# First two tiles of five stages multiplied before the input is normalised

## The reference

```python
def rms_norm(x, g, eps=NORM_EPS):
    xf = x.astype(jnp.float32)
    y = xf * lax.rsqrt(jnp.mean(xf * xf, axis=-1, keepdims=True) + eps)
    return (y * g.astype(jnp.float32)).astype(x.dtype)

for l in range(DEPTH):
    x = x + 0.5 * swiglu(rms_norm(x, ffn_norm[l, 0]), ...)      # ffn0, ffn2
    p = rms_norm(x, mix_norm[l]) @ w_in[l]                      # att_in, rec_in
    ...
    x = x + jnp.concatenate([ya, yb, yc], axis=-1) @ w_out[l]   # mix_out
    x = x + 0.5 * swiglu(rms_norm(x, ffn_norm[l, 1]), ...)      # ffn1, ffn3
```

## Time and profile before

| what | value |
| --- | --- |
| median of 3 runs | 3910.22 us (3909.51 to 3916.24) |
| profiled execution | 3910.8 us, its span 3909.0 us |
| mean granted TensorE clock | 0.946 |
| PE busy | 3678.5 us (94%) |
| DVE, ACT, POOL busy | 1465.1, 1211.4, 1237.4 us (37%, 31%, 32%) |
| matmuls of L1642 to L1644 on h, 2736 each | 1079.5, 1067.0, 1067.2 us busy |

### The profile page before, as it was taken

The page is one execution under the profiler, slowest core; times in us unless marked ns, Lnnn a source line. Parts: engine busy times, 40 slices in busy tenths (PEclk is TensorE's granted clock), DMA queues, the critical chain, the costliest instruction groups (busy, mean ns, idle before and its releaser), DMA issues.

```text
span 3909.0 us, 47618 instructions
## 1 busy us (share of the span) xinstructions
PE 3678.5 (94%) x17904; PEld 3033.3 (78%) x17904; DVE 1465.1 (37%) x2601; ACT 1211.4 (31%) x1800; POOL 1237.4 (32%) x516
## 2 busy tenths in 40 slices
PE   8999997689999999999768999989899999989999
PEld 7888775578888888877558888877677888778887
DVE  4430496753330333039565333122454221222110
ACT  3222335223222322233533322222323332323331
POOL 3444330003444344433000244423101444323443
PEclk9999997799999999999768999989999999999999
DMA  4442220003442344222000244322101222212222
GB/s 171 145 145 91 71 81 6 1 1 117 143 145 101 124 145 145 92 71 81 11 1 1 94 144 145 108 76 74 39 6 44 92 97 97 70 54 86 97 97 92
DMA packets 93534, 332.09 MB, mean 85 GB/s; under 512 B 10432, under 2 KB 12128, under 8 KB 93280
## 3 DMA queue, kind: packets, MB, share of 16 engines
q1 hardware_dynamic: 77136, 274.65, 20.3%
q10 hardware_dynamic: 16272, 55.65, 4.2%
HBM read 327.64 MB, written 2.62 MB: 84 GB/s over the span
## 4 chain that ended last, share of the span: by engine, by line
PE 89%; DVE 6%; ACT 2%; issue 1%; DMA 1%; SPq 0%; DVEq 0%; ACTq 0%
PE ps L1642 23%; PE ps L1644 22%; PE ps L1643 22%; PE ps L1676 2%; PE ps L1661 1%; PE ps L1662 1%; PE ps L1666 1%; PE ps L2347 1%; PE ps L1749 1%; DMA w_raw<-in_tiles 1%; PE ps L1901 1%; PE ps L2332 1%; PE ps L1742 1%; PE ps L2080 1%; PE ps L2062 1%
## 5 line engine op out<-in xcount | busy, mean ns | idle before, releaser
L418 POOL TENSOR_TENSOR w_lo<-w_raw,w_hi 128x1024 fp32r<-128x1024 f32 x512 | 1237.2, 2418 | 2648.3 <-ACT w_hi L440 2647.9
L1642 PE MATMUL ps<-h_hi,w_hi 128*128 128x512 f32 x2736 | 1079.5, 395 | 9.0 <-DVE mem L1529 7.0
L1644 PE MATMUL ps<-h_hi,w_lo 128*128 128x512 f32 x2736 | 1067.2, 390 | 0.0
L1643 PE MATMUL ps<-h_lo,w_hi 128*128 128x512 f32 x2736 | 1067.0, 390 | 0.0
L440 ACT ACTIVATE w_hi<-w_raw 128x1024 fp32r<-128x1024 f32 x512 | 541.7, 1058 | 1121.1 <-DMA w_raw<-in_tiles 1121.0
L1642 PEld LDWEIGHTS ps<-h_hi,w_hi 128*128 128x128 f32 x2736 | 514.8, 188 | 130.8 <-issue 14.7
L1643 PEld LDWEIGHTS ps<-h_lo,w_hi 128*128 128x128 f32 x2736 | 514.8, 188 | 108.4 <-issue 3.8
L1644 PEld LDWEIGHTS ps<-h_hi,w_lo 128*128 128x128 f32 x2736 | 514.6, 188 | 108.5
L1009 DVE TENSOR_TENSOR a_lo<-sil,a_hi 128x512 f32 x132 | 275.6, 2088 | 468.4 <-ACT a_hi L516 468.4
L1642 PE MATMUL ps<-a_hi,w_hi 128*128 (+1 forms) x1056 | 415.0, 393 | 0.0
L1643 PE MATMUL ps<-a_lo,w_hi 128*128 (+1 forms) x1056 | 414.3, 392 | 0.0
(11 more groups left out here) (418 smaller groups left out, 3756.5 us busy)
## 6 DMA issues: line engine op xcount, KB each, us to landing
w_raw<-in_tiles SPq DMA_DIRECT2D x512, 512.0 KB, 3.2
ada_raw<-in_ada_tiles ACTq DMA_DIRECT2D x96, 512.0 KB, 3.3
x<-in_x_t SPq DMA_DIRECT2D x2, 1024.0 KB, 6.4
sq<-in_cond ACTq DMA_DIRECT2D x4, 512.0 KB, 4.2
out_t<-x SPq DMA_DIRECT2D x1, 2048.0 KB, 7.1
consts<-in_consts SPq DMA_DIRECT2D x1, 1280.0 KB, 12.6
mem<-in_ctx_t ACTq DMA_DIRECT2D x1, 1024.0 KB, 5.8
core_mem<-in_consts ACTq DMA_DIRECT2D x1, 576.0 KB, 3.7
```

The source lines that it names most:

```text
L418: nc.gpsimd.tensor_tensor(w_lo[:, s, :], w_raw[:, s, :], w_hi[:, s, :].bitcast(F32), ALU.subtract).then_inc(S["w_lo_ready"], 1)
L1642: nc.tensor.matmul(bank, wh, hi, start=first, stop=False, skip_group_check=True)
L1643: nc.tensor.matmul(bank, wh, lo, start=False, stop=False, skip_group_check=True)
L1644: return nc.tensor.matmul(bank, wl, hi, start=False, stop=last, skip_group_check=True)
```

## The change

In att_in0, ffn1, ffn2, att_in1 and ffn3, tiles 1 and 2 are multiplied with x times gain, split in hi and lo but without the norm's factor (`raw_tiles`). ACT makes the hi part (`raise_raw`), DVE the lo part (`lower_raw`), for the first chunks early: four in the middle of the down half of the stage before, or six among the tiles of mix_out. After a feed-forward stage they lie in h_hi and h_lo, after mix_out in a part of a_lo. The sum of the last chunk comes after the first raw chunk, the spreading of the factor after the third. The factor is copied to SBUF, and the normalised h is made beside the raw products, for tiles 3 and 4, which now run side by side. The raw results are scaled afterwards: in a feed-forward stage by two products of DVE around the silu, in attention by one product for each tile. In ACT's loop over h_hi, tile 5 is rounded after the fifth chunk and tile 6 after the seventh. Not shown below: the new semaphores, and the slot of `sil`, which goes by the position of a chunk and no longer by its number.

```diff
@@ -294,6 +294,33 @@
+RAW_NEXT = {"ffn0": "att_in0", "mix_out0": "ffn1", "ffn1": "ffn2", "ffn2": "att_in1", "mix_out1": "ffn3"}
+RAW = {after: name for name, after in RAW_NEXT.items()}
+def raw_parts(name):
+    if RAW[name].startswith("ffn"):
+        return h_hi, h_lo
+    return a_lo[:, 6:6 + KD, :], a_lo[:, 6 + KD:6 + 2 * KD, :]
+def raw_order(name):
+    return FFN_ORDER if RAW[name].startswith("ffn") else tuple(range(KD))
+def raw_gain(name, k):
+    n = int(name[-1])
+    return param("ffn_g" if name.startswith("ffn") else "mix_g", KD * n + k)
+def raw_rstd(name):
+    return mem[:, 27 if name.startswith("ffn") else 47, :]
@@ -450,6 +478,34 @@
+    def raise_raw(name, k):
+        nc.scalar.activation(raw_parts(name)[0][:, k, :], x[:, k, :], ACT.Copy, scale=raw_gain(name, k)).then_inc(S["raw_hi"], 1)
+    def norm_raw(name, updates):
+        order, base = raw_order(name), BASE[name]
+        for n in range(seen.pop("early"), KD):
+            square_x(n, order[n], updates)
+        todo = order[seen.pop("raw_early"):]
+        for k in todo[:len(todo) // 2]:
+            raise_raw(name, k)
+        act.wait_ge(S["ss_ready"], seen["sq_slot"])
+        nc.scalar.activation(rtok[:, :], ps[:, 7, 0:TB], ACT.Sqrt, scale=1.0 / D, bias=eps(EPS_NORM)).then_inc(S["std_ready"], 1)
+        for k in todo[len(todo) // 2:]:
+            raise_raw(name, k)
+        for t in seen.pop("late_tiles"):
+            round_tile(t)
+        for n, k in enumerate(order):
+            act.wait_ge(S["hf_ready"], due("hf_ready"))
+            if n < KD - 1:
+                act.wait_ge(S["raw_used"], due("raw_used"))
+            else:
+                act.wait_ge(S["w_used"], base + 2)
+            nc.scalar.activation(h_hi[:, k, :], sil[:, n % 2, :], ACT.Copy).then_inc(S["h_hi_ready"], 1)
+            if n in (4, 6):
+                round_tile(base + 4 + (n - 4) // 2)
@@ -466,31 +522,38 @@
-    def round_out(base, updates):
+    def round_out(base, updates, after=None):
...
                 square_x(k - 1, k - 1, updates + 1)
+                if after:
+                    raise_raw(after, k - 1)
+        seen["raw_early"] = KD - 2
...
     def ffn(n, order, updates, shift=None):
-        base = BASE[f"ffn{n}"]
-        norm_x(order, updates, shift=shift)
+        name = f"ffn{n}"
+        base, raw, after = BASE[name], name in RAW, RAW_NEXT.get(name)
+        if raw:
+            norm_raw(name, updates)
+        else:
+            norm_x(order, updates, shift=shift)
@@ -500,20 +563,31 @@
                 nc.scalar.activation(row, row, ACT.Silu).then_inc(S["cond_ready"], 1)
-        with act.Fori(0, NF // 2) as i:
+        def pairs(i):
...
-                act.wait_ge(S["w_used"], base + 4 * i + (2 * j + 2))
+                from_raw = raw and isinstance(i, int) and j == 0
                 act.wait_ge(S["a_ready"], NF * n + 2 * i + (j + 1))
-                nc.scalar.activation(sil[:, j, :], ps[:, 2 * j, :], ACT.Silu).then_inc(S["silu_ready"], 1)
-                round_tile(base + 4 + 2 * j, i)
-                round_tile(base + 5 + 2 * j, i)
+                if from_raw:
+                    act.wait_ge(S["raw_scaled"], due("raw_scaled"))
+                    nc.scalar.activation(sil[:, 0, :], sil[:, 0, :], ACT.Silu).then_inc(S["silu_ready"], 1)
+                else:
+                    act.wait_ge(S["w_used"], base + 4 * i + (2 * j + 2))
+                    nc.scalar.activation(sil[:, j, :], ps[:, 2 * j, :], ACT.Silu).then_inc(S["silu_ready"], 1)
+                    round_tile(base + 4 + 2 * j, i)
+                    round_tile(base + 5 + 2 * j, i)
...
+        if raw:
+            pairs(0)
+        with act.Fori(int(raw), NF // 2) as i:
+            pairs(i)
@@ -533,7 +607,10 @@
                 square_x(c, FFN_ORDER[c], updates + 1)
-            seen["early"] = KD // 2
+            if after:
+                for c in range(KD // 2):
+                    raise_raw(after, FFN_ORDER[c])
+            seen["early"] = seen["raw_early"] = KD // 2
@@ -564,8 +641,9 @@
             act.wait_ge(S["w_used"], base + m + 1)
-            nc.scalar.activation(mem[:, att_unit(m), :], ps[:, m % 2, :], ACT.Copy).then_inc(S["proj_out"], 1)
-            round_tile(base + m + 4)
+            nc.scalar.activation(mem[:, att_unit(m), :], ps[:, 4 + m if m < 2 else m % 2, :], ACT.Copy).then_inc(S["proj_out"], 1)
+            if m >= 2:
+                round_tile(base + m + 4)
@@ -775,7 +853,7 @@
         round_h(range(4, KD))
-        round_out(BASE[f"mix_out{l}"], updates)
+        round_out(BASE[f"mix_out{l}"], updates, RAW_NEXT[f"mix_out{l}"])
@@ -969,17 +1047,32 @@
-    def norm_x(gain, shift=None):
+    def lower_raw(name, k):
+        hi, lo = raw_parts(name)
+        dve.wait_ge(S["raw_hi"], due("raw_hi"))
+        nc.vector.scalar_tensor_tensor(lo[:, k, :], x[:, k, :], raw_gain(name, k), hi[:, k, :].bitcast(F32), ALU.mult, ALU.subtract).then_inc(S["raw_lo"], 1)
+    def norm_x(gain, shift=None, raw=None):
+        todo = raw_order(raw)[seen.pop("raw_early"):] if raw else ()
+        for k in todo[:len(todo) // 2]:
+            lower_raw(raw, k)
...
         nc.vector.reciprocal(rtok[:, :], rtok[:, :]).then_inc(S["rtok_ready"], 1)
+        for k in todo[len(todo) // 2:]:
+            lower_raw(raw, k)
...
+        rstd = raw_rstd(raw) if raw else ps[:, 7, :]
+        if raw:
+            link(nc.vector.tensor_copy(rstd, ps[:, 7, :]))
         def make(k, slot):
-            return nc.vector.scalar_tensor_tensor(slot, x[:, k, :], gain(k), ps[:, 7, :], ALU.mult, ALU.mult)
-        split_h(range(KD), make, shift)
+            return nc.vector.scalar_tensor_tensor(slot, x[:, k, :], gain(k), rstd, ALU.mult, ALU.mult)
+        split_h(raw_order(raw) if raw else range(KD), make, shift)
@@ -995,16 +1088,25 @@
     def ffn(n, gain, shift, gate):
-        base = BASE[f"ffn{n}"]
-        norm_x(gain, shift)
+        name = f"ffn{n}"
+        base, raw, after = BASE[name], name in RAW, RAW_NEXT.get(name)
+        norm_x(gain, shift, name if raw else None)
...
             for j in range(2):
-                dve.wait_ge(S["silu_ready"], NF * n + 2 * i + (j + 1))
-                nc.vector.tensor_tensor(sil[:, j, :], sil[:, j, :], ps[:, 2 * j + 1, :], ALU.mult).then_inc(S["af_ready"], 1)
+                if raw and isinstance(i, int) and j == 0:
+                    dve.wait_ge(S["h_ready"], seen["h_hi_ready"])
+                    dve.wait_ge(S["w_used"], base + 2)
+                    nc.vector.tensor_tensor(sil[:, 0, :], ps[:, 0, :], raw_rstd(name), ALU.mult).then_inc(S["raw_scaled"], 1)
+                    dve.wait_ge(S["silu_ready"], NF * n + 1)
+                    link(nc.vector.tensor_tensor(sil[:, 0, :], sil[:, 0, :], ps[:, 1, :], ALU.mult))
+                    nc.vector.tensor_tensor(sil[:, 0, :], sil[:, 0, :], raw_rstd(name), ALU.mult).then_inc(S["af_ready"], 1)
+                else:
+                    dve.wait_ge(S["silu_ready"], NF * n + 2 * i + (j + 1))
+                    nc.vector.tensor_tensor(sil[:, j, :], sil[:, j, :], ps[:, 2 * j + 1, :], ALU.mult).then_inc(S["af_ready"], 1)
@@ -1014,7 +1116,9 @@
                 activations(i, 2)
-        with dve.Fori(both, NF // 2) as i:
+        if raw:
+            activations(0, 1)
+        with dve.Fori(max(both, int(raw)), NF // 2) as i:
@@ -1034,7 +1138,10 @@
+            if half and after:
+                for k in FFN_ORDER[0:KD // 2]:
+                    lower_raw(after, k)
+        seen["raw_early"] = KD // 2
@@ -1063,13 +1170,18 @@
-        norm_x(lambda k: param("mix_g", KD * l + k))
+        norm_x(lambda k: param("mix_g", KD * l + k), raw=f"att_in{l}")
...
         first = seen.get("proj_out", 0)
-        dve.wait_ge(S["proj_out"], first + 1)
+        dve.wait_ge(S["proj_out"], first + 2)
+        rstd = raw_rstd(f"att_in{l}")
+        for unit in (U_KI, U_MISC):
+            ins = nc.vector.tensor_tensor(mem[:, unit, :], mem[:, unit, :], rstd, ALU.mult)
+        ins.then_inc(S["raw_evened"], 1)
+        dve.wait_ge(S["raw_evened"], l + 1)
@@ -1473,6 +1585,9 @@
             V.tensor_tensor(x[:, k, :], x[:, k, :], ps[:, (k - 1) % KD, :], ALU.add).then_inc(S["x_ready"], 1)
+            if 0 < k < KD - 1:
+                lower_raw(RAW_NEXT[f"mix_out{l}"], k - 1)
+        seen["raw_early"] = KD - 2
@@ -1683,14 +1798,46 @@
         seen["early"] = 0
+        spread_rstd()
+    def spread_rstd():
...
+    def raw_tiles(name, banks):
+        (hi, lo), t = raw_parts(name), BASE[name]
+        for n in range(seen.get("early", 0), KD - 1):
+            sum_chunk(n)
+        pe.wait_ge(S["w_lo_ready"], t + 2)
+        for n, k in enumerate(raw_order(name)):
+            block = slice(k * P, (k + 1) * P)
+            pe.wait_ge(S["raw_hi"], due("raw_chunk"))
+            for r in range(2):
+                nc.tensor.matmul(ps[:, banks[r], :], w_hi[:, (t + r) % RING, block], hi[:, k, :], start=(n == 0), stop=False, skip_group_check=True)
```

(37 more changed lines are left out.)

13 lines of the change are left out of this document (7 added, 6 removed).

## The result

| what | before | changed |
| --- | --- | --- |
| median | 3911.52 us (3909.51 to 3917.66, 7 runs) | 3929.29 us (3923.93 to 3944.55, 7 runs) |
| ratio | | 1.0049, 95% interval 1.0033 to 1.0065 |
| profiled execution, its span | 3910.8, 3909.0 us | 3944.55, 3942.8 us |
| mean granted TensorE clock | 0.946 | 0.940 |
| PE busy | 3678.5 us | 3700.4 us |

The change made the kernel 0.5% slower. The forecast of 3917.6 us had the sign and the place; its size was off by 11.7 us, and its range ended at 3926. The profiled execution above is the slowest of its seven, so the places are read here by their durations and not by the difference of the spans.

The account below looks back on a forecast made before the run. The prediction took PE as the bound, 89% of the span. Attention's −5.6 and the feed-forward stages' +13.0 gave +7.4 us on the profiled 3910.8, 0.6 above the median: 3917.6 for the median, range 3901 to 3926.

Parts of the forecast that it names:

- last h_hi: Feed-forward stages: ACT begins the last rounded chunk of h 10.05 us after E, the end of tiles 1 and 2.
- tiles 3 and 4 end: PE ends them at E + 12.65: 10.9 us of products and 1.75 of waiting for h_lo of chunk 7.
- pair 3: Feed-forward tiles 5 and 6 start at E + 17.6, after pair 1's product is read; PE idles for 5 us.
- The collision of the last `make` with POOL: DVE's last normalised chunk, held by POOL's subtraction, ends at E + 10.0; from PSUM it would be E + 8.3.
- Rivals 1 and 2: First: DVE and POOL don't collide, 3902 us, chance 0.15. Second: PE is the only bound, 3888 us, chance 0.07.
- The clock among the sums: At each boundary, three sums in a row lower PE's clock: 1.5 us lost, bounds 0 and 3.4.
- As at the old boundaries I take 1.7: Feed-forward stages: PE's clock falls after its idle time before pair 3, costing 1.7 us, bounds 0 and 2.8.
- The sums inside the down halves: Rows of four sums in the feed-forward down halves: no added time was forecast for them.
- The attention stages: att_in0 and att_in1: tile 5 comes 3.4 us sooner, less 0.6 of clock: gain 2.8 each, 5.6 for both.
- the 0.6 us of clock behind the short waits: Attention stages: two short PE waits may lower the clock once in three times, 0.6 us, bounds 0 and 1.7.
- Rival 4: Clock down another turn in feed-forward stages, or condition row delayed: +2 in each, +0.5 elsewhere, 3925 us; chance 0.12.
- Rival 3: Fewer sums in a row at the boundaries no longer lower the clock: 7.5 us back, net 0, 3910 us; chance 0.14.

Follow-up runs that it names:

- e1: Changed kernel, with the products that make the normalised chunks reading the factor from PSUM and not from its SBUF copy: 3926.41 us, ratio to before 1.0021.
- e2: Changed kernel, with ACT rounding tiles 5 and 6 behind the eight chunks of h and not between them: 3910.11 us, ratio to before 0.9976.
- e10: Changed kernel, with the boundary's last two sums set behind the first and second raw chunk, the factor's spread behind the fourth: 3927.21 us, ratio to before 1.0023.
- e11: Changed kernel, with four useless PE products behind tiles 3 and 4 of each raw feed-forward stage: 3928.61 us, ratio to before 1.0027.
- e3: Changed kernel, with the condition row's load issued behind the norm's root and not behind the eight chunks: 3921.03 us, ratio to before 1.0010.
- e6: e4, with the last two sums at each of the five boundaries set between the raw chunks: 3898.16 us, ratio to before 0.9962.
- e8: e6, with the four sums of each down half also set between four down tiles: 3883.89 us, ratio to before 0.9920.
- e12: e8, with the factor spread behind the third raw chunk instead of the fourth: 3883.00 us, ratio to before 0.9906.
- e5: Changed kernel, with raw tiles kept at att_in0 and att_in1 alone, the feed-forward stages as before: 3919.19 us, ratio to before 1.0003.
- e4: Changed kernel with three edits: factor from PSUM, tiles 5 and 6 rounded behind the chunks, condition row loaded early: 3900.41 us, ratio to before 0.9951.
- e7: Kernel before, with the down half's four sums in a row set one behind each of four down tiles: 3909.92 us, ratio to before 0.9985.

## Why the prediction was wrong

The order of events was right to 0.5 us. Forecast and profile, from E, in the feed-forward stages: last h_hi 10.05, found 10.3; tiles 3 and 4 end 12.65, found 13.0 to 13.1; pair 3 at 17.6, found 17.58 to 17.62. The collision of the last `make` with POOL, which the Trainium skill (SBUF — State Buffer, "Who interferes with whom") let one expect, is there at its forecast size (2.76 us; the forecast had 2.4), and e1 and e2 show it from two sides: a `make` from PSUM is not held, and one that POOL does not meet is not either. Rivals 1 and 2 fell with that.

What failed are the three terms of the clock. They make 13.3 of the 13.8 us between +7.4 and +21.2:

- **"The clock among the sums", 1.5 us for each boundary.** At T the clock went to half for 6.8 us and not for 3.4, in four of five boundaries (E − T 18.6 against 17.1). That is 1.5 each, 6.0 us: 4.5 in the feed-forward stages, 1.5 in att_in1. The upper bound of 3.4 held it, but I chose the value nearest to one row with four sums (ffn0's), where the old boundaries, about 10 us at half clock, stood in the same profile. e10 takes this term away: E − T 15.5.
- **"As at the old boundaries I take 1.7" for the restart behind the wait.** It was 2.6, 2.3 and 2.6 us (13.5, 13.2 and 13.5 less 10.9), 2.5 more in all; e11 shows that it is the wait that costs it.
- **The sums inside the down halves**, 4.8 us, weren't in the sum at all: the forecast put them at nothing, as no line of the change touches these sums. In both profiles of the changed kernel their dip is twice as long in ffn1, ffn2 and ffn3. Why stays open, and it isn't shown that the change causes it: e1, e3, e10 and e11 have the same code there and show 0, 3.4 or 6.8 us.

The attention stages gained 2.6 and 1.1 us where 2.8 each was forecast, and 1.5 of the difference is the first term in att_in1. The forecast had rightly moved the rotation and the transposes to the other side of tile 5. That att_in0 came within 0.2 us is luck in part: the 0.6 us of clock behind the short waits never came (the grant is 1.00 over tiles 3 to 6 of both attention stages), while tile 5 was 0.3 us later from E than forecast, and the rotations and transposes in a row behind it took half a us more than in their old places.

Sum: 6.0 + 2.5 + 4.8 + 0.4 (the rest of the attention stages) + 0.1 = 13.8, and 7.4 + 13.8 = 21.2. Rival 4 had the right mechanism ("the clock stays down for another turn") and nearly the right price for the boundaries, 7.4 + 7.0 = 14.4 where they show 16.4. Its chance of 0.12 was too small, and the range held nothing for the down halves: with the boundaries alone the time would be 3910.2 + 16.4 = 3926.6, at its edge. Rival 3, that the sums don't bring the clock down, was tested the other way round: with two in a row they don't (e6, e8, e10, e12, all 20 boundaries), with three they do in 36 of 37 (the boundaries with raw tiles in the changed kernel twice, e1 to e5 and e11). Between the two kinds the spread of the factor moved by one chunk as well; the clock falls ahead of it, 2.3 to 4.1 us from T, where the spread comes at 9.3 or later, so it isn't the cause.

The reading of the loss itself, that ACT's ordered loop and not the raw products costs the time, is confirmed by e4: with the three obstacles out of the loop the scheme is 19 us faster than the kernel before (12.5 us at the boundaries).

## What to carry to other kernels

Where work is moved into an engine's in-order loop, list what the loop waits for and what queues behind it: here two roundings set between eight chunks cost more than everything the change gained, and moving two lines (e2) won 29 to 32 us back. Price every new idle time of TensorE and every row of one-column products twice, for itself and for the slow products behind it, and set narrow products singly between dense ones. Compare two programs at the same matmul of both; a time to "the start of tile 5" is another quantity when something was moved across it.

## What the runs showed of the hardware

- **Sums in a row and the clock.** The sum of a chunk is eight one-column products, in which PE counts as fully busy: 3.40 us of 3.40 in rows 4. Behind four in a row the grant is 0.58 over 4.0 us; one behind each down tile leaves it at 1.00 (e7). Three at a boundary were followed by half clock for 3.4 to 10.2 us in 36 of 37 places, two by none in 20.
- **How long a dip lasts is not a property of the place.** In the eleven profiles with four sums in a row in the down halves, these were followed by 3.4 us at half clock, by 6.8, or, in 5 of the 55 places, by none. In ffn1, ffn2 and ffn3: 3.4 each before and in e4 and e5; 6.8 each in both profiles of the changed kernel; 3.4, 0, 0 in e1; 3.4, 6.8, 3.4 in e2; 3.4, 0, 6.8 in e3; 6.8, 6.8, 3.4 in e6; 6.8, 0, 6.8 in e10; 3.4, 3.4, 0 in e11. One such place in e1 (ffn2), the sums and what follows:

```profile
1631.44:1644.56 13.12, 13.12 (x75) 11.51 (x75) 2.74 (x4) 5.15 (x9) 4.22 (x2) 1.00 0.26 81
```

  What decides is open, and it was read in one profile of each kernel (two of the changed one).
- **Who gets the port.** When POOL had two subtractions queued back to back, DVE's waiting one got in between: 2.48 us for DVE and 5.20 for POOL's pair, which take 4.83 alone.
- **Attention takes one of several times whatever the edit.** From the first product of tile 7 to the next feed-forward stage's T the fourteen profiles take 477.5 to 486.9 us in layer 0 and 481.9 to 492.5 in layer 1. The kernel before had 477.9 and 488.3, the changed one 479.8 and 492.3, then 482.6 and 481.9. It mostly goes with the time at half clock in it, from 123 us in the shortest to 147 in the longest, and differs from about 150 us after that part's start. Before, and then e5:

```profile
612.00:656.00 44.00, 37.25 (x239) 26.98 (x238) 35.91 (x78) 22.29 (x62) 0.00 (x0) 0.92 0.00 1
```

```profile
612.00:656.00 44.00, 39.48 (x212) 29.35 (x214) 30.52 (x67) 19.46 (x52) 0.00 (x0) 0.77 0.00 1
```

  Few and short products run there, and in the same 44 us one executes 239 and the other 212. What sets it off was not tried. With the down halves it is the likely reason, not tested, why the runs of one kernel spread over up to 20 us and why the ratios above stand up to 10 us off the boundaries' sums.
